# Byte offsets of the matmul operands in SBUF: inputs 192, outputs 128 bytes of 256 from the weights

## The reference, cut to what matters

```python
def swiglu(h, w_gu, w_down):
    gate, up = jnp.split(h @ w_gu, 2, axis=-1)
    return (jax.nn.silu(gate) * up) @ w_down

for l in range(2):
    x = x + 0.5 * _swiglu(_rmsnorm(x, ffn1_norm[l]), ffn1_w_gate[l], ffn1_w_up[l], ffn1_w_down[l])
    h = _rmsnorm(x, mix_norm[l])
    ...
    x = x + merged @ w_out[l]
    x = x + 0.5 * _swiglu(_rmsnorm(x, ffn2_norm[l]), ffn2_w_gate[l], ffn2_w_up[l], ffn2_w_down[l])
mem_n = rmsnorm(mem, norm_mem)
for i in range(4):
    x = x + mix                      # diff_attention, hgrn2, chunked_sgu, diff_attention of rmsnorm(x)
    x = x + mem_cross_attention(rmsnorm(x, norm_cross[i]), mem_n, ca_w_q[i], ca_w_kv[i], ca_w_o[i])
    x = x + swiglu(rmsnorm(x, norm_ffn[i]), ffn_w_gu[i], ffn_w_down[i])
return rmsnorm(x, norm_final)
```

## The kernel before

| tensors | before | after |
|---|---|---|
| raw, wl, wh, x | 0 | 0 |
| ah, al, full, mh, ml, con with decays, ones | 0 | 192 |
| gh, gl, oh, ol, soh, sol, hoh, hol, lh, ll, qf, kf, vt, prob2, pt2, kc, vc, memn | 192 | 128 |

## Time and profile before

### The profile page before, as it was taken

How to read it: one execution, slowest core, us unless ns; L and a number is a source line. 1 busy time by engine, 2 the same in 40 slices (tenths; PEclk the granted TensorE clock), 3 DMA queues, 4 the chain that set the end, 5 groups by cost and what they waited for, 6 DMA issues and landing times.

```text
span 2962.0 us, 55892 instructions
## 1 busy us (share of the span) xinstructions
PE 2899.1 (98%) x24180; PEld 2848.7 (96%) x24180; DVE 1072.8 (36%) x1883; ACT 1324.9 (45%) x1476; POOL 2110.9 (71%) x462
## 2 busy tenths in 40 slices
PE   8999999999999999999999999999999999999998
PEld 8999889999999899999999998999999999999998
DVE  3316543323155442335332145332124331353321
ACT  5344534344345444345443475443354433454432
POOL 6777557878876568875778873668876588766785
PEclk9999989999999899999999999999999999999999
DMA  8964335555554354554445542445554455544453
GB/s 233 194 202 156 129 128 183 181 192 185 186 173 150 113 185 171 188 179 146 157 166 181 195 171 72 157 157 185 185 199 145 146 181 192 176 144 156 171 185 114
DMA packets 74197, 496.88 MB, mean 168 GB/s; under 512 B 8399, under 2 KB 13135, under 8 KB 14968
## 3 DMA queue, kind: packets, MB, share of 16 engines
q1 hardware_dynamic: 68344, 485.88, 45.8%
q10 hardware_dynamic: 5632, 7.62, 2.7%
HBM read 490.05 MB, written 3.41 MB: 167 GB/s over the span
## 4 chain that ended last, share of the span: by engine, by line
PE 88%; POOL 3%; issue 2%; DVE 2%; DMA 2%; ACT 2%; SPq 0%; POOLq 0%; DVEq 0%
PE G L447 21%; PE G L448 21%; PE G L449 21%; PE S L447 6%; PE S L449 6%; PE S L448 6%; POOL wl L396 3%; DMA raw<-w_units 2%; PE G L653 1%; PE S L1003 1%; ACT wh L1074 1%; PE S L528 1%; PE S L802 0%; PE S L765 0%; PE S L759 0%
## 5 line engine op out<-in xcount | busy, mean ns | idle before, releaser
L396 POOL TENSOR_TENSOR wl<-raw,wh 128x2048 fp32r<-128x2048 f32 x458 | 2110.7, 4619 | 821.7 <-ACT wh L1074 800.8
L1074 ACT ACTIVATE wh<-raw 128x2048 fp32r<-128x2048 f32 x456 | 872.6, 1916 | 1115.1 <-DMA raw<-w_units 1112.1
L447 PE MATMUL G<-ah,wl 128*128 128x256 f32 x4304 | 1229.9, 286 | 12.2 <-DVE wl L1721 8.6
L448 PE MATMUL G<-al,wh 128*128 128x256 f32 x4304 | 1223.2, 284 | 0.0
L449 PE MATMUL G<-ah,wh 128*128 128x256 f32 x4304 | 1222.9, 284 | 0.0
L447 PEld LDWEIGHTS G<-ah,wl 128*128 128x128 f32 x4304 | 831.8, 193 | 20.1 <-issue 15.3
L448 PEld LDWEIGHTS G<-al,wh 128*128 128x128 f32 x4304 | 831.7, 193 | 0.4
L449 PEld LDWEIGHTS G<-ah,wh 128*128 128x128 f32 x4304 | 831.5, 193 | 0.0
L447 PE MATMUL S<-gh,wl 128*128 128x256 f32 x1408 | 390.1, 277 | 3.3 <-POOL wl L396 3.3
L448 PE MATMUL S<-gl,wh 128*128 128x256 f32 x1408 | 389.9, 277 | 0.0
L449 PE MATMUL S<-gh,wh 128*128 128x256 f32 x1408 | 389.9, 277 | 0.0
(11 more groups left out here) (367 smaller groups left out, 3806.8 us busy)
## 6 DMA issues: line engine op xcount, KB each, us to landing
raw<-w_units SPq DMA_DIRECT2D x459, 1024.0 KB, 4.8
bias<-tables ACTq DMA_DIRECT2D x24, 128.0 KB, 3.2
tables<-trow ACTq DMA_DIRECT2D x12, 192.0 KB, 9.1
con<-consts SPq DMA_DIRECT2D x1, 1056.0 KB, 16.6
x<-x_in SPq DMA_DIRECT2D x4, 256.0 KB, 5.5
raw<-w_units SPq DMA_DIRECT2D x4, 256.0 KB, 6.2
memx<-mem_in ACTq DMA_DIRECT2D x1, 1024.0 KB, 5.5
out<-full SPq DMA_DIRECT2D x4, 256.0 KB, 2.5
```

Of the source, the lines that this page charges most:

```text
L396: pool.tensor_tensor(wl[:, j * UW:(j + 1) * UW], raw[:, j * UW:(j + 1) * UW], wh[:, j * UW:(j + 1) * UW].bitcast(F32), ALU.subtract)\
L447: pe.matmul(out, sl, vh, start=start and k == 0, stop=False, **kw)
L448: pe.matmul(out, sh, vl, start=False, stop=False, **kw)
L1074: act.activation(wh[:, j * UW:(j + 1) * UW], raw[:, j * UW:(j + 1) * UW], ACT.Copy)\
```

## The change

The change places 192 unused bytes between x and ah. It halves ones from 256 to 128 columns, which makes room for them. It adds a line that rounds the start of work up to 128 bytes of 256 from raw. The scan of the forget gates, which had read 256 columns of ones, reads one column broadcast over 256. All other instructions of all engines are the same, in the same order, with the same shapes.

```diff
     at[0] = (at[0] + 63) // 64 * 64
+    raw_at = at[0]
     raw = sb("raw", RING * UW)
     wl = sb("wl", RING * UW, F32R, offset=at[0] - 4 * RING * UW)
     wh = sb("wh", RING * UW, F32R)
     x = sb("x", KD * T)
+    at[0] += 192
     acts_at = at[0]
     ah = sb("ah", KD * T, F32R)
...
     con = sb("con", NCONST)
-    ones = sb("ones", T)
+    ones = sb("ones", P)
     pick2 = sb("pick2", 28)
     root = sb("root", 4 * T + 8)
     rr = root[:, 3 * T:4 * T + 2]
     small = sb("small", 136)
+    at[0] += (raw_at + 128 - at[0]) % 256
     work_at = at[0]
     WORK = 12288
     work = sb("work", WORK)
...
-                dve.tensor_tensor_scan(summed, ones[0:4, 0:T], fbank, 0.0, ALU.mult, ALU.add)\
+                dve.tensor_tensor_scan(summed, ones[0:4, 0:1].to_broadcast([4, T]), fbank, 0.0, ALU.mult, ALU.add)\
                     .then_inc(vec_step, c.one(vec_step))
```

## The result

The changed kernel took **2934.54 us** in the median of four runs (2927.72 to 2940.82), the kernel before 2966.09 (2964.68 to 2971.71) beside it. The ratio is 0.9889, with a 95% interval of 0.9874 to 0.9904. It is faster, as forecast, but by 31.5 us where 88 were expected, and 2934.5 lies above the range (2836 to 2918). The profiled execution took 2931.57 us.

A forecast was written before the change was run, and what follows sets the result against it. The prediction took the rate of TensorE's own matmul stream to bound the kernel. Against the profiled 2964.1 us its terms gave -95 + 7 - 8 + 0 + 8 = -88, so 2876 us, range 2836 to 2918.

The forecast's parts named there:

- Bound: Whole kernel: only the rate of TensorE's own stream, busy 2899 of 2962 us, can be worth much.
- Part 1: Products moving ah, al, mh, ml go to distance 192: 14200 x 6.7 ns, -95 us, with +7 us given back.
- from the down stage, the same helper at the distance that these get: Source of the input products' price: 6.7 ns between the steady values 120.0 and 113.3.
- one in ten: Share of input products expected at 118.0 instead of 113.3 ns, giving back +7 us.
- Part 2: Token products, activations stationary and weights moving, go to distance 64: 1920 products, 4 to 13 us gain, taken as -8 us.
- Part 3: Gated products and mixer outputs, 5760 in all, go to distance 128: no change, 0, with ends -25 and +38 us.
- The bound of +38: Worst end for outputs at distance 128: the spacing of distance 0, 120 ns, 5760 x 6.6 ns.
- Part 4: Waits for VectorE or ScalarE in ten mixer and cross-attention stages lengthen: +8 us given back, ends 0 and 20.
- the inputs settle at 118: Rival: long gate and up stages take 118 ns because they are entered from other streams; 2935 us, chance 0.10.
- Distance 128 is as bad as 0: Rival on gated products and mixer outputs: 2876 + 38 = 2914 us, chance 0.08.
- Distance 128 reaches the 109 ns: Rival on gated products and mixer outputs: they reach 109 ns spacing, 2876 - 25 = 2851 us, chance 0.14.
- the place isn't what matters: Rival: the low memory area may be slow for its own reason, so nothing changes; 2964 us, chance 0.05.

The follow-up runs named there:

- the outputs alone: Changed kernel with the inputs put back at distance 0 and the work area left at 128: 2992.59 us, ratio 1.0086 to the kernel before.
- the best version: Inputs and outputs at 192, two extra distance-0 matmuls ahead of stretches in feed-forward blocks, mixers, cross-attention and behind the memory's sums: 2886.52 us, ratio 0.9746.
- the inputs alone: Changed kernel with inputs kept at distance 192 and the work area put back at 192: 2918.26 us, ratio 0.9831 to the kernel before.
- a burst of four: Four extra distance-0 matmuls ahead of each feed-forward stage's third unit, results unused: 2891.04 us with inputs and outputs at 192, 2954.57 us with both at 64.

## Why the prediction missed its range

- **Bound.** Right. TensorE's rate of starts sets the time; the differences above add up to the span's within 0.1 us, and the busy times of GpSimd, ScalarE and VectorE stayed.
- **Part 1, inputs at 192: -95 and +7 forecast, -55 measured** (-48.3 for ah, -6.8 for mh). The direction and the pair of values were right; no third value came up. The step that failed is the price "from the down stage, the same helper at the distance that these get", with "one in ten" at 118. Nearly half of the products took 118. This part is 33 of the 55 us by which the forecast missed. Some 25 of the 33 are the rhythm: at the full clock the mean spacing of these products fell from 120.0 to 115.5 ns, over 14211 of them 63 us instead of 88. Some 4 are the clock, for 194 of them start at 1.2 GHz (about 214 ns) where 156 did, and 5 are waits, which lie in these rows too. The differential stages at 118 were read as an exception. They were the other case of a choice that is made again at each entry.
- **Part 2, tokens: -8 forecast, -6.9 measured.** Right, and for its reason: both rhythms occur at distance 64, 617 of the 1920 at 113 and 1260 at 118.
- **Part 3, outputs at 128: 0 forecast, +27.7 measured** (+21.3 and +6.4). This step failed. I took no change as "nearest to the rows at 64 and 192", though both are 64 bytes away from a multiple of 256, while 128 lies 128 away and no row is at 128. Distance 128 gives stretches of 118.7 to 120 ns in the mean, nearly the worst; single starts at 113 are mixed in, but no stretch of them. The bound of +38 was right, and with the outputs alone the kernel is slower by 26 us. That run also shuts out that the loss came from faster stages ahead.
- **Part 4, given back: +8 forecast.** The row of all other matmuls grew by 1.9 us. TensorE's idle time on the page, which has the waits of all rows, grew by 4.0 (span less busy time, 62.9 before and 66.9 after). Either is within the ends. The waits below grew by 0.5 us for pt and not at all for pb. GpSimd stayed cover: the waits for its wl in the down stages are 2.8 us after, 3.3 before, and 4.6 us in the best version, whose long stages all run at 113.

```profile
PE G L656 <- DVE pt L1982: 9.3, 4, 3.9
PE S L762 <- DVE pb L2110: 3.8, 4, 0.9
```

Put together by the rows of the table (the last term is the 1.9 us against 8): 2876 + 33 + 28 + 1 - 6 = 2932, and the profiled execution took 2931.6.

**The rivals.** The time came out beside "the inputs settle at 118" (2935), but not for its reason: half of them did, and distance 128 took the rest. My ground against that rival, that all eight down stages run at 113 though "entered straight from the gate products", doesn't hold. They do so behind gate products at 120. Behind a stage at 118 they run at 118. "Distance 128 is as bad as 0" was nearly right in its price (28 of 38 us), and no case combined the two, which is why the range ended at 2918 (added up as it says, 2914 and half of the 12 us from +8 to 20, it would be 2920; the measurement lies above both). "Distance 128 reaches the 109 ns" is out; that bound came from transposes of 128 columns, and no long stretch of products in any run was under 113.3. So is "the place isn't what matters": the kernel with slots 32 bytes apart changes the spacing from unit to unit with the slot, and a shift by 256 bytes changes nothing. The rule of the Trainium skill ("TensorE: Matmul & The Clock Gate", "What happens when you issue a matmul", step 1) that the two operands come through independent read ports would leave no room for that. Here the measurement decides against it as a rule for the rate of starts.

**What stays open.** The runs show that at distance 192 the entry chooses between 113 and 118 by the number of matmuls and the rhythm that comes in, and that the choice lasts for 960 products and over the border to the next stage. I take that for a phase between the weight loads and the moving reads, but no record shows either read, so the mechanism isn't shown. The counts above are a rule for this kernel's row sums and for nothing else. What sets the rhythm behind the first block's four small matmuls or behind other breaks in the mixers isn't known, nor why the sums turn it over at 192 and not at 64.

## What to carry to other kernels

Where a stream of fp32r products with a weight load each bounds the kernel, read its spacing by start times in each stage, not by mean durations, and compare it with the distance of moving and stationary operands modulo 256. A value seen at one place is one of several that a stream can hold, so list every stage at that distance before pricing all by it. A distance that no row shows may be the worst one, so try parts of such a change apart: here the inputs alone are better than the whole (2918 against 2935 us), and a few matmuls ahead of each long stretch brought 27 us more. Where such matmuls are tried, try several numbers and note the rhythm that comes in: two kept it, three turned it over, and four set it.

## What I had not expected of the hardware

- The spacing of 256-column products against the distance, at the full clock: 120.0 ns at 0, 116.7 at 32 in the long stretches, 113.3 or 117.8 at 64, 118.7 to 120 at 128, 113.3 or 117.8 at 192. It doesn't fall steadily away from 0. And 64 above isn't the same as 64 below: a burst of four puts every long stretch of 960 at 113 at 192 and none at 64.
- At 192 there are two rhythms, 4.5 ns apart, and a stage hands its own to the next. 27 us hang on 32 matmuls placed ahead (2918.3 against 2891.0).
- Two fp32 sums ahead of a stream at 192 turn its rhythm over, at 44 of 44 places. With two matmuls more it stays as it came, with three it turns again (19 of 20), with four it is 113 (36 of 36). Between four and three lie 34 us (2891.0 against 2925.4).
